# An RWKV-7 block kernel: the 16x16 diagonal blocks of its triangle inverses by substitution on GpSimd, through DRAM, one head pair ahead

## The reference, cut to what matters

```python
def wkv_scan(r, w, k, v, a, b, s0):
    def step(s, inp):
        r_t, w_t, k_t, v_t, a_t, b_t = inp
        sa = jnp.einsum('dbhvk,dbhk->dbhv', s, a_t)
        s = s * w_t[..., None, :] + sa[..., :, None] * b_t[..., None, :] + v_t[..., :, None] * k_t[..., None, :]
        return s, jnp.einsum('dbhvk,dbhk->dbhv', s, r_t)
    s_final, y = lax.scan(step, s0, (r, w, k, v, a, b))
    return y, s_final
```

## Time and profile before

| | |
|---|---|
| median of 3 runs | 3312.16 us (3301.2 to 3312.37) |
| the profiled execution | 3313.88 us, its span 3312.1 us |
| PE busy over the span | 3099.8 us (94%), PEld 2572.7 (78%) |
| DVE, ACT, POOL busy | 1567.8 (47%), 733.2 (22%), 1058.2 (32%) |
| mean granted clock of TensorE | 0.961 of full speed |

### The profile page before, as it was taken

One profiled execution on the slowest core, in us unless ns is written; L12 is line 12 of the kernel. 1 busy time (PEld: TensorE's weight loads), 2 busy tenths in 40 slices (PEclk: granted clock), 3 DMA queues, 4 the chain that ended last, 5 costly groups with the idle time before them and its releaser, 6 DMA issues.

```text
span 3312.1 us, 70246 instructions
## 1 busy us (share of the span) xinstructions
PE 3099.8 (94%) x30244; PEld 2572.7 (78%) x30244; DVE 1567.8 (47%) x1977; ACT 733.2 (22%) x1079; POOL 1058.2 (32%) x482
## 2 busy tenths in 40 slices
PE   6799997999995999999999899999999999999996
PEld 0577885788784999999888688888888888888885
DVE  0667667446785445545432733333433333333336
ACT  0322222012222222222111322212121212222221
POOL 0343343443430000000034344444444444444442
PEclk7799997999997999999999999999999999999998
DMA  9665566322333111110242122222222222222222
GB/s 405 228 221 203 200 230 233 100 79 101 131 122 151 50 44 50 50 50 21 88 191 95 66 94 96 96 96 96 96 95 96 96 93 94 94 95 96 96 96 108
DMA packets 103203, 392.69 MB, mean 119 GB/s; under 512 B 15104, under 2 KB 16896, under 8 KB 96128
## 3 DMA queue, kind: packets, MB, share of 16 engines
q1 hardware_dynamic: 72288, 289.43, 24.8%
q10 hardware_dynamic: 30336, 96.64, 8.3%
q0 software_dynamic: 288, 2.10, 0.2%
HBM read 355.87 MB, written 32.26 MB: 117 GB/s over the span
## 4 chain that ended last, share of the span: by engine, by line
PE 64%; DVE 2%; issue 1%; ACT 0%; POOL 0%; ACTq 0%; DVEq 0%; POOLq 0%
PE bank L931 16%; PE bank L932 16%; PE bank L930 16%; PE bank L671 12%; PE bank L687 2%; PE bank L747 1%; PE bank L735 1%; PE bank L815 1%; PE bank L813 1%; DVE buf L1793 0%; DVE buf L1794 0%; PE bank L695 0%; DVE buf L1510 0%; DVE buf L1750 0%; PE bank L759 0%
## 5 line engine op out<-in xcount | busy, mean ns | idle before, releaser
L514 POOL TENSOR_TENSOR buf<-buf 128x1024 fp32r<-128x1024 f32 x288 | 697.2, 2421 | 1581.1 <-ACT buf L1130 1581.1
L931 PE MATMUL bank<-buf 128*128 128x512 f32 x2304 | 909.6, 395 | 0.0
L932 PE MATMUL bank<-buf 128*128 128x512 f32 x2304 | 908.0, 394 | 0.0
L930 PE MATMUL bank<-buf 128*128 128x512 f32 x2304 | 903.4, 392 | 0.5 <-POOL buf L514 0.3
L1130 ACT CAST buf<-buf 128x1024 fp32r<-128x1024 f32 x288 | 302.7, 1051 | 1263.8 <-PE bank L932 1261.8
L930 PEld LDWEIGHTS bank<-buf 128*128 128x128 f32 x2304 | 433.0, 188 | 104.4 <-issue 1.9
L931 PEld LDWEIGHTS bank<-buf 128*128 128x128 f32 x2304 | 432.5, 188 | 101.4 <-issue 0.5
L932 PEld LDWEIGHTS bank<-buf 128*128 128x128 f32 x2304 | 432.6, 188 | 95.7
L671 PE MATMUL bank<-buf 64*64 64x64 f32 x13248 | 430.6, 220 | 26.4 <-issue 13.9
L538 PE MATMUL bank<-buf 128*128 128x512 f32 (+1 forms) x1168 | 431.7, 370 | 21.3 <-POOL buf L508 14.2
L671 PEld LDWEIGHTS bank<-buf 64*64 64x64 f32 x13248 | 413.8, 137 | 38.7 <-issue 34.3
(11 more groups left out here) (214 smaller groups left out, 2380.0 us busy)
## 6 DMA issues: line engine op xcount, KB each, us to landing
buf<-stream SPq DMA_DIRECT2D x382, 512.0 KB, 3.3
buf<-adarows ACTq DMA_DIRECT2D x108, 512.0 KB, 5.1
buf<-ada SPq DMA_DIRECT2D x32, 1024.0 KB, 13.0
scaled_keys<-buf ACTq DMA_DIRECT2D x18, 768.0 KB, 5.8
buf<-scaled_keys SPq DMA_DIRECT2D x18, 768.0 KB, 7.0
buf<-adarows SPq DMA_DIRECT2D x20, 512.0 KB, 6.9
buf<-tokens SPq DMA_DIRECT2D x4, 1536.0 KB, 21.1
buf<-bias ACTq DMA_DIRECT2D x6, 1024.0 KB, 6.2
```

Of the source, the lines that this page charges most:

```text
L514: G.tensor_tensor(wl2[b % SPLIT2], raw2[b], wh2[b % SPLIT2].bitcast(F32), ALU.subtract).then_inc(split2, 1)
L930: pe.matmul(bank[:, :], lh, rh, start=start, stop=False)
L931: pe.matmul(bank[:, :], lh, rl, start=False, stop=False)
L932: return pe.matmul(bank[:, :], ll, rh, start=False, stop=stop)
```

## The change

Levels 1, 2, 4 and 8 of the inversion leave TensorE. The 16x16 diagonal blocks of each triangle are inverted by substitution on GpSimd instead, and TensorE keeps the two levels 16 and 32 (15 blocks). The way of a pair's triangles is now:

1. TensorE makes `lowT` (3 blocks) and `low` (1.5 blocks: one direction only) in a new step `lows(j + 1)`, which stands at the head of iteration j, before `inverse(j)`; three steps of the chain stand between its blocks. VectorE masks them into LT and LG.
2. SP stores LG (384 KB) and LT (768 KB) to DRAM, waits, and gathers the 16x16 blocks with 16 DMAs into Y. Each moves 12 x 16 rows of 16 numbers, 64 bytes each.
3. GpSimd runs 30 dependent steps on Y: a memset, 14 times a multiply and an add, and a transposing copy to YT.
4. SP stores the inverted blocks with 32 such DMAs into two DRAM images (zeros elsewhere), waits, and loads X and XT (768 KB each) whole.
5. `inverse(j + 1)` waits for both in iteration j + 1.

The loads of a pair and this moving of blocks stand in one program order on SP. The diff, cut to that:

```diff
-LEVELS = [2, 4, 8, 16, 32]
+LEVELS = [16, 32]
+BASE = 16
+SUB_STEPS = 2 + 2 * (BASE - 2)
+CHAIN_BESIDE_LOWS = {1: 1, 2: 2, 4: 3}
+VARIANCE_BEHIND = 5
...
@@ SP
-            for j in range(BPAIRS):
+            def load_pair(j):
                 if j:
-                    ready(sp, ("low", j - 1, 2))
+                    ready(sp, ("tA", j - 1, 2), ("rk", j - 1, 1))
                 if j > 1:
                     ready(sp, ("rc", j - 2, 1))
...
-                for n, dst in enumerate((AH, BH, KH)):
-                    sp.dma_start(dst, hatd[j, n]).then_inc(R["load"], 16)
+                sp.dma_start(AH, hatd[j, 0]).then_inc(R["ab"], 16)
+                sp.dma_start(BH, hatd[j, 1]).then_inc(R["ab"], 16)
+                sp.dma_start(KH, hatd[j, 2]).then_inc(R["load"], 16)
...
                 if j > 1:
                     sp.wait_ge(R["done"], j - 1)
                 sp.dma_start(late[j % 2], valued[j, :, TOK:]).then_inc(R["late"], 16)
+            def move_blocks(j):
+                ready(sp, ("lowT", j, 0), ("lowT", j, 1), ("lowT", j, 2), ("low", j, 0), ("low", j, 1))
+                sp.dma_start(lowd, LG).then_inc(R["lg"], 16)
+                sp.dma_start(lowtd, LT[j % 2]).then_inc(R["lg"], 16)
+                sp.wait_ge(R["lg"], 32 * (j + 1))
+                for h, q, d in itertools.product(range(2), range(4), range(2)):
+                    sp.dma_start(group(Y, h, q, d), block(lowtd, h, q, 1) if d else block(lowd, h, q, None)).then_inc(R["yl"], 16)
+                sp.wait_ge(R["sub"], 1 + SUB_STEPS * (j + 1))
+                sp.wait_ge(R["img"], 32 + 512 * j)
+                sp.wait_ge(R["xl"], 32 * j)
+                for h, q, d in itertools.product(range(2), range(4), range(2)):
+                    sp.dma_start(block(ximg, h, q, d), group(YT if d else Y, h, q, d)).then_inc(R["img"], 16)
+                    sp.dma_start(block(xtimg, h, q, d), group(Y if d else YT, h, q, d)).then_inc(R["img"], 16)
+                sp.wait_ge(R["img"], 32 + 512 * (j + 1))
+                if j:
+                    ready(sp, ("inv", j - 1, NX - 1))
+                sp.dma_start(X, ximg).then_inc(R["xl"], 16)
+                if j:
+                    ready(sp, ("z", j - 1, 2), ("w", j - 1, 2))
+                sp.dma_start(XT, xtimg).then_inc(R["xl"], 16)
+            load_pair(0)
...
+            move_blocks(0)
+            for j in range(1, BPAIRS):
+                load_pair(j)
+                move_blocks(j)
@@ GpSimd
+            for j in range(BPAIRS):
+                pool.wait_ge(R["yl"], 256 * (j + 1))
+                step(G.memset(Y[0:96, :].rearrange("p (h e) -> p h e", h=2)[:, :, 0:BASE * BASE:BASE + 1], 1.0))
+                for k in range(1, BASE - 1):
+                    rows, shape = BASE - 1 - k, [96, 2, BASE - 1 - k, k]
+                    part = product[0:96, 0:2 * rows * k].rearrange("p (h r s) -> p h r s", h=2, r=rows)
+                    step(G.tensor_tensor(part, a[:, :, k + 1:, k:k + 1].to_broadcast(shape), a[:, :, k:k + 1, 0:k].to_broadcast(shape), ALU.mult))
+                    step(G.tensor_tensor(a[:, :, k + 1:, 0:k], a[:, :, k + 1:, 0:k], part, ALU.add))
+                step(G.tensor_copy(at.rearrange("p h r s -> p h s r"), a))
@@ TensorE
+            def lows(j, n):
+                pe.wait_ge(R["ab"], 32 * (j + 1))
...
             for j in range(BPAIRS):
+                for n in range(5):
+                    if j + 1 < BPAIRS:
+                        lows(j + 1, n)
+                    if j and n in CHAIN_BESIDE_LOWS:
+                        chain(j - 1, CHAIN_BESIDE_LOWS[n])
                 inverse(j)
                 for g in range(3):
                     ready(pe, ("invT", j, NX - 3 + g), ("gv", j, g), ("tA", j, g))
                     blocks(("z", j, g), XT, GV, g)
                     blocks(("w", j, g), XT, AT, g)
-                if j:
+                    if j and g == 0:
+                        read(j - 1)
+                    if j and g == 1:
+                        mean(j - 1)
+                if j + 1 < BPAIRS:
+                    front(j + 1, j - 1 if j else None)
+                elif j:
                     variance(j - 1)
-                if j + 1 < BPAIRS:
-                    front(j + 1)
@@ ScalarE
-            start_inverse(0)
@@ VectorE
-                    elif name == "lowT":
-                        dve.wait_ge(R["xi"], 2 * j + 2)
-                        V.tensor_tensor(wide(LT, g), four(use(dve, key)), over(0), ALU.mult)
-                        placed(key, XT, 3, g)
-                    elif name == "low":
-                        placed(key, X, 2, g)
-                    if out is not None and (name, g) == ("gk", 2):
+                    if out is not None and (name, g) == ("rb", 1):
                         normed(out)
                     if out is not None and (name, g) == ("rk", 1):
                         gated(out)
```

More of the change, by code:

```diff
@@ L12 @@
+import itertools
 from contextlib import ExitStack
@@ L109, in bank_uses, with front @@
     add = lambda key, bank, reader: order.append((key, bank, reader))
-    def front(j):
-        for (name, g), bank, reader in TURN_GRAM:
+    def front(j, out=None):
+        for n, ((name, g), bank, reader) in enumerate(TURN_GRAM):
             add((name, j, g), bank, reader)
+            if out is not None and n == VARIANCE_BEHIND:
+                add(("var", out), 6, "s")
     def values(j):
@@ L121, in chain @@
             add(("chain", j, n, d), 6 + d, "v")
+    def lows(j, n):
+        if n < 3:
+            add(("lowT", j, n), 3 + n, "v")
+        else:
+            add(("low", j, n - 3), n - 1, "v")
+    for n in range(5):
+        lows(0, n)
     front(0)
@@ L132, in bank_uses @@
                 add(("invT", j, x - 1), 4 + (x - 1) % 2, "v")
[L133 to L138, removed]
+            if j:
+                chain(j - 1, 4 + x)
         for g in range(3):
@@ L696, in turned_values, with lows, front @@
                 mm.then_inc(full(key), 1)
-            def front(j):
-                pe.wait_ge(R["load"], 16 + 80 * (j + 1))
-                for (name, g), _, _ in TURN_GRAM:
+            def lows(j, n):
+                pe.wait_ge(R["ab"], 32 * (j + 1))
+                if n < 3:
+                    blocks(("lowT", j, n), BH, AH, n)
+                else:
+                    key = ("low", j, n - 3)
+                    bank = fill(key)
+                    for i in range(8 if n == 3 else 4):
+                        for hs in heads:
+                            mm = pe.matmul(bank[hs, T * i:T * i + T], AH[hs, inst(8 * (n - 3) + i, 0)], BH[hs, inst(8 * (n - 3) + i, 0)],
+                                           start=True, stop=True)
+                    mm.then_inc(full(key), 1)
+            def front(j, out=None):
+                pe.wait_ge(R["load"], 16 + 48 * (j + 1))
+                for n, ((name, g), _, _) in enumerate(TURN_GRAM):
                     key = (name, j, g)
@@ L715, in front @@
                         turned(key, dict(tA=AH, tB=BH, tK=KH)[name], g)
+                    if out is not None and n == VARIANCE_BEHIND:
+                        variance(out)
             def values(j):
@@ L765, in inverse @@
                     if x < NX:
[L766 to L769, removed]
+                        ready(pe, ("invX", j, x - 3) if l else ("lowT", j, g))
+                        if x == 0:
+                            pe.wait_ge(R["xl"], 32 * (j + 1))
+                        blocks(("inv", j, x), LT[j % 2], X, g)
                     if x:
@@ L790, in pe_core @@
             pe.wait_ge(F["gatec"], BPAIRS)
-            pe.wait_ge(R["load"], 96)
+            for n in range(5):
+                lows(0, n)
             front(0)
@@ L1138, in group, with front @@
                 return a[:, 512 * g:512 * g + width]
[L1140 to L1145, removed]
-                nc.scalar.copy(XT.rearrange("p (u n) -> p u n", n=T), units).then_inc(R["xi"], 1)
-            def front(j):
-                for (name, g), _, reader in TURN_GRAM:
+            def front(j, out=None):
+                for n, ((name, g), _, reader) in enumerate(TURN_GRAM):
                     if reader == "s":
@@ L1557, in centred @@
                 V.scalar_tensor_tensor(yc, use(dve, key)[:, :], -1.0 / HD, Ys, ALU.mult, ALU.add).then_inc(copy_done(key), 1)
-            dve.wait_ge(R["load"], 96)
+            dve.wait_ge(R["load"], 64)
+            for n in range(5):
+                lows(0, n)
             front(0, None)
             for j in range(BPAIRS):
+                if j == 0:
+                    dve.wait_ge(F["hst"], 64 * BPAIRS)
+                    dve.wait_ge(F["ost"], 16 * BPAIRS)
+                for n in range(5):
+                    if j + 1 < BPAIRS:
+                        lows(j + 1, n)
+                    if j and n in CHAIN_BESIDE_LOWS:
+                        chain(j - 1, CHAIN_BESIDE_LOWS[n])
                 for x in range(NX + 1):
```

133 lines of the change are left out of this document (86 added, 47 removed).

## The result

| | before | after |
|---|---|---|
| median of 4 runs, us | 3309.41 (3301.2 to 3312.37) | 3350.69 (3347.31 to 3354.46) |
| ratio | 1 | 1.0129, 95% interval 1.0106 to 1.0152 |
| profiled execution, us | 3313.88 | 3349.49 |
| its span, granted clock | 3312.1, 0.961 | 3347.3, 0.932 |

The change makes the kernel slower by 1.3%, 41 us; on a second chip the ratio was 1.0109 (1.0088 to 1.0129). The forecast was 3371 us in 3290 to 3480, slower.

What follows compares the result with a forecast made beforehand. TensorE paced the old 96.7 us iteration; SP's wait and the moving would then bound it: 3 + 55 + 6 + 9 + 14 + 18 + 10 = 115 us. With start and end, 59.2 us later: 3371 us, range 3290 to 3480.

Steps and rivals of the forecast that it cites:

- What leaves TensorE: TensorE, each iteration: 28.5 blocks of `inverse` and `low` go, 26.6 us; if it still paced, 70.1 us instead of 96.7.
- The wait on SP: SP's queue: the load of `late` waits for `gated` ahead of the stores of LG and LT, 55 us into each iteration.
- The moving: Stores, gather, POOL steps, block stores and loads run serially behind SP's wait: 57 us per iteration.
- gather, 16 DMAs: SP's gather of diagonal blocks into Y: 16 issues at 0.42 us plus 2.3 for landing, 9 us (7.6 to 21).
- 30 steps on POOL: Substitution on GpSimd: 5.3 us products and sums, 1.2 copy, 7.5 fixed parts, 14 us (9.5 to 20).
- 32 stores: SP's stores of inverted blocks to DRAM, in 64-byte pieces: 18 us, near the issue pace of 12.9.
- The clock: TensorE at the head of each iteration: after idling, four blocks at the lower clock cost 3 us more (0 to 4).
- The sum: Whole kernel: start, iterations and end put the core's end 59.2 us later, 3373.1 us profiled, 3371 as median.
- Each us is worth 6: The moving stands six times in the total (start, pair 1, four iterations), so each us of it counts six.
- The moving that hides as meant: Rival, core: moving begins once triangles are masked, fits in 63 us under TensorE's 70.1; 3197 us, chance 0.05.
- Issues were neither at 1.2 us: Rival, SP's small DMAs: at 1.2 us an issue, gather 21 and stores 40 us; 3575 us, chance 0.10.
- the DMAs queue one after the other: Rival, SP's 12 KB DMAs: without overlap 48 take 110 us instead of 27; 3870 us, chance 0.02.

Runs made afterwards that it cites:

- e5: As e1, and SP's wait for `rc` of pair j-2 moved to directly ahead of RH's load; two runs, 3200.97 and 3203.31 us, ratios 0.9667 and 0.966.
- e1: Changed kernel with the load of `late` and its wait for `gated` put behind the moving of that pair's triangles; 3211.37 us, ratio 0.9681.
- e2: Changed kernel with each product on GpSimd computed three times, 28 steps more; 3418.92 us, ratio 1.0298.
- e6: Changed kernel in its own order without the 32 stores of inverted blocks; 3270.45 us, ratio 0.9863.
- e3: Changed kernel without the 28 products and sums on GpSimd, memset and copy kept; 3297.57 us, ratio 0.9929.
- e7: The changed kernel itself, unaltered, run again on a second chip; 3351.58 us, ratio 1.0109.

## Why the prediction was right, point by point

- **What leaves TensorE.** 26.6 us of blocks per iteration were forecast; PE's busy time fell from 92.8 to between 66.4 and 67.5, 25 to 26 us. TensorE's own pace was put at 70.1; the two e5 runs have 70.3 to 73.1, since more of it is idle between blocks. Behind the moving this cost nothing.
- **The wait on SP.** This was the step the forecast rested on, and e1 shows it as the cause: without it the kernel gains 4.4%. The load of `late` was issued 54.6 us into iteration 1 (1245.37 less 1190.75), against 55; the work of PE and DVE ahead of it was counted rightly. One sign was read off wrongly: SP was to wait 40 to 50 us at L502 each time, and it waited 61 (244.2 in 4). The wait begins before the iteration does: SP issued RH's load at 1295.13 us, iteration 2 began at 1301.92, and the 55 us come on top.
- **The moving.** From SP's timeline and POOL's, term by term in iteration 1:

| term | forecast | measured | from |
|---|---|---|---|
| to the load of `late` | 55 (58 with the clock) | 54.6 | 1190.75 to 1245.37 |
| issue, stores of LG, LT | 6 | 7.7 | to 1253.09 |
| gather, 16 DMAs | 9 | 10.8 | to 1263.92 |
| 30 steps on POOL | 14 | 12.9 | to 1276.79 |
| 32 stores | 18 | 15.4 | to 1292.14 |
| loads of X, XT, AH, BH | 10 | 9.8 | to 1301.92 |
| sum | 112 (115) | 111.2 | |

The sum of the moving behind L502, 56.6 us against 57, is closer than its terms are, and that is luck: the first stores and the gather took 3.5 us more, the steps on POOL, the 32 stores and the last loads 3.9 less. On POOL a step has a fixed part of 0.27 us against 0.25, and a number costs 1.8 ns against 2.4.

- **The clock.** The 3 us added at the head of iterations 2 and 3 were too much. The lower level is there: at the head of iteration 2 the clock granted was 0.50 (1.2 GHz), then 0.80.

```profile
1301.92:1306.00 4.08, 4.08 (x76) 4.08 (x78) 1.05 (x2) 0.00 (x0) 0.00 (x0) 0.50 0.84 340
1306.00:1310.00 4.00, 4.00 (x118) 4.00 (x116) 2.85 (x9) 0.00 (x0) 0.00 (x0) 0.80 0.00 0
```

But iteration 1, where the forecast saw PE barely idle and added nothing, began on that level too: after 6.24 us of idling the clock granted in its first 4 us was 0.50, and the first 64 products took 3.68 us, as in iterations 2 and 3. The load of `late` still came after 54.6 us; in iteration 2 it came after 55.3 (1357.17 less 1301.92). What was mis-sized is clock and stalls together: the forecast's work is 51.9 us, so 2.7 are left for both in iteration 1, where 3 were kept for stalls and, from iteration 2 on, 3 more for the clock. An estimate of the clock's part: the first `inv` began at 1197.59, 6.8 us into the iteration, and 4.5 blocks and three chain steps at full clock make 4.9, so some 2 us.
- **The sum, too high by 23.6 us** (3373.1 against 3349.49 in profiled executions). At `lows(2)` the forecast was 4.7 us late (1195.5 against 1190.75); iterations 1 to 3 took 332.0 instead of 342, 10.0 less, of which 6 are the clock's 3 us twice and the rest the steps on POOL and the 32 stores, less what the first stores and the gather took more; the stretch to `inverse(5)` took 108.1 instead of 112; and from there to the core's end 49.0 instead of 53.4. Together 23.1.
- **"Each us is worth 6".** This holds upward (e2: 71.6 us for 11.6 a pair); downward it is 5 at most (e6: 72.9 for 15.5; e3: 51.1 for some 11.6). The forecast's own numbers had it, PE ready at 1193.5 and the moving at 1195.5, but the sentence did not draw the conclusion.
- **The rivals.** The moving that hides as meant (3197 us) would have been right but for SP's order: e5, with both waits out of the way, has 3201 and 3203. That the numbers are this close is in part luck: `lows(2)` began at 1189.81 us in e5_rc_behind and not at 1195.5, and its iterations took 72.8 and not 70.1. Issues were neither at 1.2 us nor did the DMAs queue one after the other: in the changed kernel issues of 12 KB followed each other every 0.44 us (16 pairs of L528 and L529 from 1276.79 to 1290.04, 0.88 us a pair). The Trainium skill (DMA: Bandwidth & Descriptors, Anatomy of one DMA) gives a fixed cost of some 2 us for a DMA issued by GpSimd. The DMAs here are issued by SP, and their traces show that a latency of that kind does not add up over transfers in flight on one queue: 32 stores took 15.4 us, their issues 14 of them, and SP waited only 1.2 us behind the last one. Whether SP or the queue sets the 0.44 us was not tried.

## What to carry to other kernels

An in-order queue carries every wait in it to all that stands behind, so before adding work that waits more than it moves to a queue, list the waits ahead of it and what each one guards; a wait that was free while only loads stood behind it becomes the bound of the new chain. Move each wait to directly ahead of the one transfer whose buffer it guards: here two such moves turned 1.1% slower into 3.3% faster on one chip (e7 and e5_rc_behind), nearly all of it by the first (e1, 0.9681). And count at each place whether the chain or the other engine ends last there, in both directions: what costs when lengthened need not pay when shortened (pair 1's moving here).

## What was unexpected of the hardware

- A step on POOL that waits for its predecessor's semaphore has a small fixed part: 0.24 us for 28 numbers per partition and 0.39 for 112, so some 0.19 us beside 1.8 ns a number, and 0.08 us from the end of one to the start of the next.
- The gather's 16 transfers took 9.4 us to issue, and POOL began 1.4 us behind the last issue (1262.53 to 1263.92): the landing of small pieces costs little once they are under way together.
- TensorE's granted clock was 0.50 in the first 4 us after an idle time of 6.24 us (iteration 1) as well as after one of 42.85 (iteration 2).
- When TensorE is relieved of a quarter of its work and not held up by loads, short idle stretches put down to "issue" stand out in its timeline, up to 3.50 us each in e5_rc_behind. They make most of the difference between 70 us per iteration and the 71 to 73 measured; their cause stays open.
